# Router logits with the router's weights stationary and the tokens moving, turned back by a product with the identity

## What is computed

```python
h2 = _rmsnorm(x, g_ffn).reshape(B * N, D)          # D = 1024
lg = (x @ w_rg + b_rg)                             # 4 group logits per token
grp = argmax(lg); p_grp = softmax(lg)[grp]
le = (x @ w_re + b_re).reshape(T, 4, 8)            # 32 expert logits per token
top_v, top_i = top_k(le[grp], 2)
gate = softmax(top_v) * p_grp
# the selected (token, expert) pairs are then sorted by expert and computed in blocks
```

## Time and profile before

| | us |
|---|---|
| time, median of 3 runs | 1685.47 (1684.23 to 1685.77) |
| profiled execution: span from first to last instruction | 1681.4 |
| PE busy | 1519.8 (90%) |
| DVE busy | 1050.2 (62%) |
| ACT busy | 880.8 (52%) |
| router stage of the second pass, from its first router product to the last bias add | 642.06 to 654.53 |
| block 1 ends, block 2 starts | about 972.4 |

### The profile page before, as it was taken

One profiled execution on the slowest core, in us unless ns is written; L12 is line 12 of the kernel. 1 busy time (PEld: TensorE's weight loads), 2 busy tenths in 40 slices (PEclk: granted clock), 3 DMA queues, 4 the chain that ended last, 5 costly groups with the idle time before them and its releaser, 6 DMA issues. The chain is left out here.

```text
span 1681.4 us, 25555 instructions
## 1 busy us (share of the span) xinstructions
PE 1519.8 (90%) x8198; PEld 1272.6 (76%) x8198; DVE 1050.2 (62%) x1523; ACT 880.8 (52%) x1187; POOL 352.3 (21%) x492
## 2 busy tenths in 40 slices
PE   6999999999999998999999923999999999999980
PEld 5888899988889998888899912666766666666660
DVE  4665444536644443565444543888988888888863
ACT  4644433355444334644433313777777777777752
POOL 1212111002221110112121022223222222322223
PEclk9999999889999997999999856999999999999995
DMA  6224343322334333224333255999999999999966
GB/s 223 76 89 165 104 139 124 109 96 87 104 141 150 114 101 140 85 83 163 116 113 127 76 178 192 383 374 372 375 382 374 376 378 380 377 373 379 382 214 234
DMA packets 72849, 355.14 MB, mean 211 GB/s; under 512 B 10881, under 2 KB 11154, under 8 KB 48034
## 3 DMA queue, kind: packets, MB, share of 16 engines
q1 hardware_dynamic: 58562, 313.72, 50.6%
q0 software_dynamic: 9824, 25.28, 6.4%
q10 hardware_dynamic: 4368, 14.94, 2.3%
HBM read 326.09 MB, written 28.28 MB: 211 GB/s over the span
## 5 line engine op out<-in xcount | busy, mean ns | idle before, releaser
L1169 DVE TENSOR_TENSOR wlo<-est,whi 128x2048 fp32r<-128x2048 f32 x193 | 440.4, 2290 | 110.9 <-ACT whi L1165 84.1
L1165 ACT ACTIVATE whi<-est 128x2048 fp32r<-128x2048 f32 x193 | 368.4, 1916 | 146.4 <-DMA est<-wexp 104.5
L718 DVE TENSOR_TENSOR w<-stage,w 128x1024 fp32r<-128x1024 f32 x175 | 224.3, 1309 | 79.9 <-ACT w L482 78.1
L482 ACT ACTIVATE w<-stage 128x1024 fp32r<-128x1024 f32 x175 | 178.5, 1054 | 126.4 <-PE ps L959 116.4
L1524 PE MATMUL ps<-whi,xT 128*96 128x512 f32 x512 | 205.6, 401 | 21.7 <-DVE xT L1474 21.7
L1526 PE MATMUL ps<-whi,xT 128*96 128x512 f32 x512 | 203.5, 398 | 0.0
L1525 PE MATMUL ps<-wlo,xT 128*96 128x512 f32 x512 | 202.6, 396 | 0.0
L957 PE MATMUL ps<-w,hT 128*128 128x384 f32 x576 | 199.1, 346 | 0.0
L959 PE MATMUL ps<-w,hT 128*128 128x384 f32 x576 | 193.0, 335 | 0.0
L958 PE MATMUL ps<-w,hT 128*128 128x384 f32 x576 | 192.8, 335 | 0.0
L957 PE MATMUL ps<-hT,w 128*128 128x384 f32 x408 | 141.4, 347 | 8.5 <-issue 5.0
(11 more groups left out here) (214 smaller groups left out, 2754.1 us busy)
## 6 DMA issues: line engine op xcount, KB each, us to landing
est<-wexp SPq DMA_DIRECT2D x193, 1024.0 KB, 13.1
stage<-wmix SPq DMA_DIRECT2D x175, 512.0 KB, 4.2
H<-x_all SPq DMA_DIRECT2D x12, 512.0 KB, 8.2
XR<-x_all SPq DMA_DIRECT2D x9, 512.0 KB, 6.0
x_scratch<-XR ACTq DMA_DIRECT2D x9, 512.0 KB, 5.4
h_scratch<-H ACTq DMA_DIRECT2D x9, 512.0 KB, 6.2
cx<-x_scratch SPq DMA_DIRECT2D x9, 512.0 KB, 7.0
y_all<-co ACTq DMA_DIRECT2D x9, 512.0 KB, 6.2
```

Source lines behind the costliest of these rows:

```text
L482: act.activation(whl[w % 2][0][:, q * PIECE:(q + 1) * PIECE], stage[r % STAGE][:], ACT.Copy)\
L718: vec.tensor_tensor(whl[w % 2][1][o], stage[r % STAGE][:], whl[w % 2][0][o].bitcast(F32), ALU.subtract).then_inc(w_lo, 1)
L1165: act.activation(whi[q][:], est[q][:], ACT.Copy).then_inc(e_hi[q], 1)
L1169: vec.tensor_tensor(wlo[q][:], est[q][:], whi[q][:].bitcast(F32), ALU.subtract).then_inc(e_lo[q], 1)
```

## The change

The router's weights become the stationary operand and the tokens' transposed values move, so that a tile's result is 36 logits x 128 tokens in columns 0 to 127 of bank j % 2. ACT copies this result to SBUF, into the first 36 partitions of a tile that is idle in this stage (`ltS`, part of `sT`; new semaphores lt_mm and lt_cp). PE turns it back by a plain product with the identity (`router_rows(j)`), with `ltS` as the stationary operand, into columns 128 to 163 of the same bank; DVE adds the bias from there. There are no more DMAs and no fewer.

```diff
+        ltS = sT[0:EXPERTS + GROUPS, :]
...
+                def lt_evac(j):
+                    act.wait_ge(lt_mm, tot(s, TPS, j + 1))
+                    act.wait_ge(log_mm, tot(s, TPS, j))
+                    act.activation(ltS, ps[0:EXPERTS + GROUPS, j % 2, 0:P], ACT.Copy).then_inc(lt_cp, 1)
+
+                h2T_evac(0)
+                h2T_evac(1)
+                lt_evac(0)
+                h2T_evac(2)
+                lt_evac(1)
+                lt_evac(2)
...
-                                      ps[:, j % 2, 0:36], rb[:], ALU.add).then_inc(log_add, 1)
+                                      ps[:, j % 2, P:P + 36], rb[:], ALU.add).then_inc(log_add, 1)
...
-                        ins = pe.matmul(ps[:, j % 2, 0:36], h2T[:, j * D + c * P:j * D + (c + 1) * P], wr[:, c, :],
-                                        start=(c == 0), stop=(c == DC - 1))
-                    ins.then_inc(log_mm, 1)
+                        ins = pe.matmul(ps[0:EXPERTS + GROUPS, j % 2, 0:P], wr[:, c, :],
+                                        h2T[:, j * D + c * P:j * D + (c + 1) * P], start=(c == 0), stop=(c == DC - 1))
+                    ins.then_inc(lt_mm, 1)
+
+                def router_rows(j):
+                    e = EXPERTS + GROUPS
+                    pe.wait_ge(lt_cp, s * TPS + (SEED + j + 1))
+                    pe.matmul(ps[:, j % 2, P:P + e], ltS, cst[0:e, C_IDENT:C_IDENT + e], start=True, stop=True).then_inc(log_mm, 1)
...
                 router_logits(0)
                 router_transposes(2)
+                router_rows(0)
                 router_logits(1)
+                router_rows(1)
                 router_logits(2)
+                router_rows(2)
```

More of the change, by code:

```diff
@@ L366, in build @@
         n2_cp = sem("n2_cp")
+        lt_mm = sem("lt_mm")
+        lt_cp = sem("lt_cp")
         log_mm = sem("log_mm")
@@ L484, in split_hi @@
                     yield
-            for k_, sm_ in ((SEED, p_cp), (SEED, silu), (SEED, qkT_cp), (SEED, z_sig), (SEED, og_act), (SEED, n2_sum),
+            for k_, sm_ in ((SEED, p_cp), (SEED, lt_cp), (SEED, silu), (SEED, qkT_cp), (SEED, z_sig), (SEED, og_act), (SEED, n2_sum),
                             (SEED, oT_hi), (SEED, mT_hi), (SEED, w_hi), (SEED, hT_hi), (SEED, gate_cp), (SEED, gate_l), (SEED, dec_e)):
@@ L613, in _, with h2T_evac @@
                 act.wait_ge(out_mm, tot(s, 3 * TPS, 3 * TPS))
-                for j in range(TPS):
+                def h2T_evac(j):
                     act.wait_ge(n2_tr, tot(s, TPS, j + 1))
@@ L968, in _ @@
             pe.wait_ge(cst_in, 16 * 2)
-            for sm_ in (tr_u, o_mm, o_tr, n1_tr, n2_tr, log_mm, proj, zr_mm, glr_mm, gate_mm, dec_mm, out_mm, score):
+            for sm_ in (tr_u, o_mm, o_tr, n1_tr, n2_tr, lt_mm, log_mm, proj, zr_mm, glr_mm, gate_mm, dec_mm, out_mm, score):
                 pe.sem_inc(sm_, SEED)
```

## The result

The changed kernel is slower: median 1690.39 us (1684.52 to 1694.42, 20 runs) against 1684.70 us of the kernel before (1681.16 to 1688.50, 20 runs), a ratio of 1.003 with the 95% interval 1.002 to 1.0039, so 3.4 to 6.6 us. Forecast were 1680.2 and a gain of 5.3 us.

What follows compares the result with a forecast made beforehand. The router stage was taken as bound by PE at half clock. Two loop turns at -4.0 and +2.7 in the last pass gave -5.3: span 1681.4 to 1676.1, with 4.07 around it 1680.2 us; range 1674 to 1689.

Steps and rivals of the forecast that it cites:

- the rival at half clock: Router stages: the clock stays at 0.50, turned products gain nothing, about +9.4 us, 1694.9; chance 0.17.
- the late rise: Router stages: the clock rises only in the middle of tile 1's products, +0.4 us, 1685.9; chance 0.15.
- 1.8 had been worked out: Router stage: the last bias add comes at 652.5 in place of 654.33, 1.8 us sooner.
- So it reaches the branch while tile 2's products run, before any store is issued.: PE's branch at the stage's end: its fetch hidden under tile 2's products and the last turn, 3.1 us.
- the 3.7 us by which PE's sequencer ran ahead: PE's branch: the sequencer ran ahead of its queue by about a tile's products, 3.7 us before the last product's end.
- up to the 2.45 of now: PE's branch: cost if its fetch is not covered, up to the present 2.45 us from last add to next pass.
- It comes at 666.6 to 669.6 in place of 672.14 ..., whatever PE's lead.: Next pass's first update product: set by ACT's return from its stores, 2.6 to 5.6 us sooner.
- The 5.3 us of the prediction: Next pass: way from ACT's return through table load, split, rotation and scaling to the update product, 5.3 us.
- the term of 2 x 4.0: The two turns of the loop: first update product 4.0 us sooner at each, -8.0 us together.
- 12 us of unbroken records: Router stage before: products with 36 moving columns never raised the clock, 0.50 for 12 us without a hole.
- the last pass: End of block 1: ACT's stores move 4.0 us, the barrier waits for them, block 2 starts 2.7 us later.
- The 1.3 us that I allowed ACT to spare: End of block 1: slack between ACT's last store issue and block 2, 1.69 less 0.4, taken as 1.3 us.

Runs made afterwards that it cites:

- e7: Changed kernel with tiles 0 and 1 turned, tile 2 in the old shape, stores on SP: 1679.93 us, ratio 0.9968 to the kernel before.
- e4: Changed kernel, stores on SP, in passes that go round held until the next pass's first gate product: 1705.09 us, ratio 1.0116 to the kernel before.
- e11: The changed kernel measured once more, unaltered: 1688.87 us against 1684.63 of the kernel before, ratio 1.0021.
- e12: The kernel before, unaltered, profiled once more as a single execution; no median or ratio given.
- e9: Changed kernel with only the last pass's six stores moved from ACT to SP: 1685.14 us against 1684.63 of the kernel before, ratio 0.9995.
- e3: Changed kernel with the six stores issued by SP behind its weight loads, not by ACT: 1680.49 us, ratio 0.9971 to the kernel before.
- e2: Kernel before, nothing turned, its six stores moved from ACT to SP behind the weight loads: 1683.49 us, ratio 0.9984 to the kernel before.
- e6: Changed kernel with only tile 0 turned, tiles 1 and 2 in the old shape, stores on SP: 1677.65 us, ratio 0.9958 to the kernel before.
- e10: As e6, with the three residual stores issued ahead of the normed ones: 1676.67 us, ratio 0.9946 to the kernel before.
- e5: Changed kernel with only tile 0 turned, tiles 1 and 2 in the old shape, stores on ACT: 1681.76 us against 1685.15, ratio 0.9983.
- e1: Kernel before, nothing turned, ACT's six stores held until behind the last router product: 1688.92 us against 1686.09, ratio 1.002.
- e8: Changed kernel with stores on SP and turn 1 placed behind tile 2's products: 1680.70 us, ratio 0.9977 to the kernel before.

## Why the prediction was wrong

**Right: pace and clock.** A product is two records, 0.21 us each at 0.50 and 0.11 at 1.00, and the turned shape gains only the clock. It rose where tile 0's products end (327.93, 645.37, 962.81), so neither the rival at half clock nor the late rise came. That it came within 0.3 us of the 645.6 is in part luck: it rose in all 30 profiled stages that turn tile 0, between 2.0 us ahead of the start of tile 0's last record and 1.1 us behind it. The last add is 1.85, 1.73 and 0.94 us sooner (336.87 to 335.02, 654.33 to 652.60, 971.91 to 970.97), the third although its pass had run 1.5 us longer (the fall at 710), since the clock rose after only 3.4 us at 0.50 there; 1.8 had been worked out.

**The step that failed first: "So it reaches the branch while tile 2's products run, before any store is issued."** I took the 3.7 us by which PE's sequencer ran ahead in the kernel before as a property of the sequencer. It is one of the program: there no wait held it at the stage's end. A turn whose operand is not there stops it, and it comes to the branch at the last turn's load (334.45, 652.02, 970.40; in e7 at turn 1's). Then the fetch, 3.4 to 4.0 us with hardly a transfer under way (e4), begins in the open, and with the stores, issued just then (651.86), it takes 4.46 and 4.88. The next pass started at 339.36 and 657.35, 0.25 and 0.57 later than before, in place of 4.0 sooner. The price put to a failed cover, "up to the 2.45 of now", was too small as well: the gap from the last add to the next pass is 4.34 and 4.75 us. And while PE stands, the clock that had just been won falls again.

**The step that failed with it: "It comes at 666.6 to 669.6 in place of 672.14 ..., whatever PE's lead."** ACT does not set the first update product; PE does. In every pass that follows a branch, of all these kernels but e4, the product comes 12.5 to 12.6 us behind the pass's first product, plus 0.48 of the time at half clock between them (1 less 0.168 / 0.325, the two spacings of the prediction): 12.55 + 0.48 x 5.85 = 15.36 before (656.78 to 672.14), 12.57 + 0.48 x 5.08 = 15.01 after (657.35 to 672.36). It was to be read ahead: in the earlier trace rows POOL's keys are ready at 670.52 (669.97 + 0.55), 1.6 us ahead of PE, and ACT's split has waited for PE's product. The 5.3 us of the prediction, put on the kernel before, would bring the product at 660.30 + 5.3 = 665.6, and it came at 672.14: the sum leaves out the waits for PE's products that the earlier trace rows show, 2.33 ahead of the split and, through ACT's copy, 2.71 ahead of the rotation. So the term of 2 x 4.0 had no ground, and with no lead of PE it came to nothing: the first update products moved by +0.04 and +0.22 us.

**Read wrongly, without effect.** The "12 us of unbroken records" at 0.50 take in tile 2's transposes; router products alone ran for 6.88 us at a stretch (32 records).

**Right in kind, too small: the last pass.** ACT's stores were to move 4.0 and block 2 2.7. Block 2 came 3.70 later (972.48 to 976.18; 4.97 by e11 and e12). The 1.3 us that I allowed ACT to spare hold: its issue ends 4.95 later (970.71 to 975.66), less 3.70 is 1.25. The size is off because the stores moved 4.95 and not 4.0: the third pass itself was 1.5 us longer, of which its stage gave a part back.

The sum of the profiled executions: first update product of the third pass +0.22, the rest of that pass +1.54, its router stage -2.70 (together the -0.94 of the last add), block 2 from 0.57 to 5.21 behind the add +4.64, from block 2 to the final norm +2.51, the final norm +0.92: +7.13, the difference between the spans. Shown by experiment is the hold of block 2 (e9 took it away) and that the turning gains once the stores are elsewhere (e3). The 1.54 are the short fall of the grant, which kernels without a turn have as well (e2, e12); the 2.51 and the 0.92 are open.

**What beats both.** Turning tile 0 alone, with the stores on SP (e6, e10), is 7.5 and 8.0 us faster than the kernel before (intervals 4.9 to 9.3 and 6.9 to 11.5 us): with tile 0 turned the clock rose in all nine stages of e5, e6 and e10, and the other two tiles ran at it without a copy, a turn or a wait, to the end in eight of the nine.

## What to carry to other kernels

Before a dependent step is put at the end of a loop body, look what stands behind it in that engine's program: the branch, and on the helping engine the transfers, wait with it, and a barrier or the next pass collects the delay. To find who sets a late instruction, compare when its operands are ready with when it starts; a gap between the two, as the 1.6 us here, says that its own engine is the reason. If a change of shape is wanted only for the clock, change just as much as makes it rise, and look in every pass whether the rest still has it at its end.

## What the runs showed of the hardware

- A taken branch of PE's loop took 3.4 to 4.0 us where the DMA share was at most 0.17 (seven branches in e1, e3, e4 and e8), 3.6 to 4.5 at 0.29 to 0.43 (e2, e7), and 4.3 to 7.8 at 0.46 and more; at the loop's end, not taken, it took 0.08. The share alone does not order them: 5.90 at 0.46 (e10), 4.46 at 0.88 (the changed kernel).
- At most 19 records still ran behind the branch's start (kernel before, e6). That is 3.4 to 3.9 us of work at 0.50 (e1, the kernel before) and 2.1 at 1.00 (e6), all the cover that an early branch had.
- In the kernel before, 32 records of the old shape ran for 6.88 us at 0.50 without a rise. In e1's second pass PE ran nothing but transposes between the grant's fall at 635.50 and its rise at 638.91, and in e4's second pass from 650.50 to 653.91.
- Once the clock was up, 32 records of the old shape took 3.76 us at 1.00 in e6; in e5's third pass the grant fell among them, 2.4 us behind the first.
- Behind the stage the grant was at 0.50 for 6.8 us in e6 and in the changed kernel, at the turns of the loop, and the next pass paid for a part: 3.1 us of these stretches fell into it in e6 and 5.1 to 6.1 in the changed kernel, at 0.48 us lost for each.
